# Restacked inputs in longer runs, input chunk 7 ahead of the taps, signed weights on GpSimd, small loads on SyncE, and identity matmuls in two waits

## The chip, the cores and the metric

The kernel runs on one NeuronCore of one Trainium2 chip. The metric is the device time of one execution in microseconds. Engines are named as in the profile: PE is TensorE, PEld its weight loads, DVE is VectorE, ACT is ScalarE, POOL is GpSimd, SP is SyncE, which here only issues DMAs.

## The reference, cut to what matters

A two-layer trunk over 256 tokens of width 1024, all in float32. Each layer is `x += mixer(rms_norm(x))`, then `x += moe(rms_norm(x))`; a final RMS norm follows.

- Layer 0's mixer is a diagonal complex state-space layer: `u = h @ w_in`; 64 groups of 16 channels with 64 complex states each; `y = real(C x) + d * u`; GELU; `g @ w_glu`, split into value and gate, `val * sigmoid(gate)`.
- Layer 1's mixer is differential attention with rotary positions: `q, k, v = h @ w_qkv`; two softmaxes per head, `attn = p0 - lam * p1`, where `lam` is a scalar, `exp(sum(lq1*lk1)) - exp(sum(lq2*lk2)) + lambda_init`, from four vectors of 64; the output of a head is RMS-normed with the gain `attn_subln_g`; then `@ w_o`.
- The MoE picks one of 4 groups and 2 of its 8 experts per token, 32 experts of width 256; gate, up and down weights of all 32 experts are read in each layer, 100 MB a layer.

## The kernel before, in words

Each engine has its own program, written out by hand in order; they meet in semaphores. An engine that waits holds up all that is behind it in its own order. SyncE issues nearly all DMAs, in one long order: inputs, state-space weights, the restacking, GLU and router weights, the expert stream of layer 0 (`whole`, L436 and L438), the eight 512-column pieces of the attention weights (`columns`, L414), the final gain (L532), then the expert stream of layer 1. Each expert unit has a slot; SyncE waits in `freed` until TensorE is done with the unit that was there. The stream of layer 0 begins when all four outputs of the state-space layer are written (`y_done` 4).

**The state-space layer.** TensorE computes u transposed in eight chunks of 128 channels (`inputs`, L1729); two chunks fill a PSUM bank. ScalarE copies a bank into SBUF in another order (`keep_u`, L685); SyncE writes it to DRAM (L449), waits, and reads it back as four loads of 64 KB into U4, each in runs of 64 elements (`restack`, L454). `drive(o)` (L1774) multiplies the transposed weights with U4, 32 recorded matmuls for each of four octets; ScalarE copies the result (`keep_x`, L398 and L399). VectorE scans: `local_states`, `carries` (both with `advance`, L1240 to L1243) and `carried` (L1284 to L1296), each for two halves; `skips` (L1249) adds the skip term to the taps' result in PSUM. `taps(o)` (L1792) multiplies the block weights with the output weights, of which `signed_c` (ScalarE, L693) makes the signed part Cb and `blocks_b` (L704) the blocks; `own` (L769) copies the taps' result into Fw. GpSimd computes eight dense weight pieces (L574 to L576), which ScalarE spreads (`spread_w2`, L780), and clears buffers (L556). The output is `y_taps` (L1834, U4 with Fw, opens the PSUM group) and `y_states` (L1841, the states with W2, closes it); then GELU (L825), a turn (L1849), a copy (L832) and the gated product `glu` (L1862).

**The attention's head.** When the last scatter of layer 0 is in PSUM, ScalarE and VectorE copy the halves of x (L624, L1511); ScalarE's `norm_raw` then makes the table of the square root resident (L625) and copies the turned x (`keep_tile`, L652). Ahead of `norm_raw` ScalarE issues five small loads: the four lambda vectors and the sub-norm gain, each to all 128 partitions (L586). TensorE runs `turn_tile` (L1681), `project(0, 0)`, `turn_tile`, `project(0, 1)`, then `turn_qk(0, 0)` (L2055), which needs VectorE's rotation (L1546 to L1550), and only then the other projections (L2045). VectorE waits for all five small loads (`s_att` 80) at L1526, ahead of its lambda arithmetic (L1528 to L1533) and the first rotation.

**The last scatter.** In layer 1 the down product of a pass (L2009, banks 6 and 7) is scattered one pass later in three bfloat16 parts (`scatter_parts`, L1974). For the last pass nothing stands between: VectorE and ScalarE split the rows (L1493 to L1502, L927 to L935), then come the scatter, the square sums (L599) and the final norm (L1069).

## Time and profile before

| | |
|---|---|
| runs | 792.18 us median of 3 (790.82 to 796.93) |
| profiled execution | 790.53 us, its span 788.7 us |
| busy, share of the span | PE 87%, PEld 51%, ACT 32%, DVE 37%, POOL 4% |
| mean granted TensorE clock | 0.95 of full |
| DMA | 238.43 MB, mean 302 GB/s |
| chain that ended last | PE 55%, SP's issues 17%, DMA 11%, DVE 9%, ACT 5% |

The profile's digits in 40 slices show where each resource works (a digit is the busy share of a slice of 19.7 us in tenths):

```profile
PE   4899999989976685686899999898989999994995
DMA  8544809979999999999990565048999932999981
```

A busy PE is not PE at its peak; its clock is either 1.2 GHz (0.50 of full) or 2.4 GHz (1.00), and a stretch with a value between has both. Idle time of an engine costs nothing unless the chain runs through it.

### The profile page before, as it was taken

Reading aid. Unit: us, or ns where it says so; the run is one execution under the profiler, and the core shown is the slowest. Engines: PE = TensorE matmul, PEld = TensorE weight load, DVE = VectorE, ACT = ScalarE, POOL = GpSimd, SP = SyncE. Lnnn points to the kernel's source line nnn. Section 1 sums busy time; section 2 is a strip of 40 time slices with the busy share of each in tenths; the row PEclk is TensorE's granted clock in tenths of the full one; section 3 lists DMA queues with packets and bytes.
Section 4 is the critical chain, followed back from the end, with each engine's and each line's share of the span. In section 5 each row is a group of like instructions: output and inputs, shape, how many; then the busy total and the mean of one; then the engine's idle time right before and its main releaser. Section 6 shows DMA issues by size and latency. Waiting matters only on the chain.

```text
span 788.7 us, 16095 instructions
## 1 busy us (share of the span) xinstructions
PE 684.7 (87%) x6372; PEld 405.5 (51%) x6372; DVE 291.6 (37%) x767; ACT 248.7 (32%) x582; POOL 35.1 (4%) x36
## 2 busy tenths in 40 slices
PE   4899999989976685686899999898989999994995
PEld 4888654555533343344444444555655655652562
DVE  6897751171111010010241535735334433331334
ACT  6686533261111011011311324533233322321224
POOL 1580000000000000000000000000000000000000
PEclk9996999999998798898999999999999999997998
DMA  8544809979999999999990565048999932999981
GB/s 225 165 134 149 230 2 396 361 308 374 418 422 420 422 419 420 421 420 411 381 385 32 214 227 199 2 179 327 421 419 422 419 162 112 423 421 420 421 338 53
DMA packets 66238, 238.43 MB, mean 302 GB/s; under 512 B 25840, under 2 KB 25984, under 8 KB 41600
## 3 DMA queue, kind: packets, MB, share of 16 engines
q1 hardware_dynamic: 65136, 237.34, 76.4%
q8 instruction: 42, 0.69, 0.3%
q10 hardware_dynamic: 1040, 0.24, 0.1%
q14 instruction: 20, 0.16, 0.1%
HBM read 235.47 MB, written 2.10 MB: 301 GB/s over the span
## 4 chain that ended last, share of the span: by engine, by line
PE 55%; SPq 17%; DMA 11%; DVE 9%; ACT 5%; issue 2%; ACTq 1%; DVEq 0%
SPq L438 14%; PE ps L1954 12%; PE ps L2045 10%; PE ps L1862 6%; PE ps L2009 6%; PE ps L1934 5%; DMA ring<-in_moe_w_up 4%; PE ps L1974 4%; DMA hT<-in_moe_w_up 4%; DMA ring<-in_moe_w_down 3%; SPq L436 3%; PE ps L2108 2%; PE ps L2119 2%; PE ps L1774 2%; PE ps L1841 1%
## 5 line engine op out<-in xcount | busy, mean ns | idle before, releaser
L1954 PE MATMUL ps<-ring,work 128*32 128x256 f32 x1504 | 126.5, 414 | 31.2 <-DMA ring<-in_moe_w_gate 11.5
L1954 PE MATMUL ps<-work 128*32 128x256 f32 x864 | 91.7, 410 | 25.1 <-DMA ring<-in_moe_w_up 7.7
L1954 PEld LDWEIGHTS ps<-ring,work 128*32 128x32 f32 x1504 | 71.2, 119 | 71.5 <-issue 50.4
L1474 DVE TENSOR_TENSOR work<-ps,work 128x256 f32<-128x256 f32 x21 | 12.9, 612 | 191.2 <-PE ps L1954 191.2
L1954 PEld LDWEIGHTS ps<-work 128*32 128x32 f32 x864 | 50.2, 118 | 56.4 <-issue 40.2
L2009 PE MATMUL ps<-ring,work 128*32 128x512 f32 x464 | 70.6, 610 | 4.7 <-issue 3.9
L1934 PE MATMUL ps<-work,xr 128*128 128x128 bf16 x736 | 66.5, 219 | 0.7 <-DVE work L1383 0.6
L1934 PE MATMUL ps<-work 128*128 128x128 bf16 x368 | 63.9, 219 | 0.0
L1934 PEld LDWEIGHTS ps<-work,xr 128*128 128x128 bf16 x736 | 57.6, 98 | 8.9 <-issue 3.3
L1862 PE MATMUL ps<-ring,work 128*128 128x512 f32 x128 | 57.1, 598 | 2.7 <-ACT work L832 2.3
L2045 PE MATMUL ps<-ring,hT 128*128 128x512 f32 x128 | 56.7, 596 | 1.8 <-ACT hT L652 1.8
L1974 PE MATMUL ps<-work 128*128 128x512 bf16 x168 | 40.4, 392 | 3.6 <-DVE work L1502 3.6
L911 ACT ACTIVATE work<-ps 128x256 f32<-128x256 f32 x21 | 13.3, 631 | 86.5 <-PE ps L1954 86.5
L1954 PE MATMUL ps<-hT,work 128*32 128x256 f32 x160 | 40.4, 410 | 0.0
L1862 PEld LDWEIGHTS ps<-ring,work 128*128 128x128 f32 x128 | 23.6, 190 | 31.0 <-issue 26.8
L2009 PE MATMUL ps<-work 128*32 128x512 f32 x176 | 36.3, 595 | 3.4 <-issue 2.5
L2045 PEld LDWEIGHTS ps<-ring,hT 128*128 128x128 f32 x128 | 23.7, 190 | 29.4 <-issue 27.1
L918 ACT COPY work<-ps 128x256 f32<-128x256 f32 x13 | 4.8, 372 | 100.2 <-PE ps L1965 100.2
L1934 PEld LDWEIGHTS ps<-work 128*128 128x128 bf16 x368 | 36.0, 98 | 0.0
L2009 PEld LDWEIGHTS ps<-ring,work 128*32 128x32 f32 x464 | 17.9, 112 | 34.2 <-issue 33.1
L896 ACT ACTIVATE work<-ps,work 128x128 f32<-128x128 f32 x92 | 26.2, 368 | 25.5 <-PE ps L1934 25.5
L1974 PEld LDWEIGHTS ps<-work 128*128 128x128 bf16 x168 | 15.7, 100 | 27.6 <-issue 7.5
(339 smaller groups left out, 1067.0 us busy)
## 6 DMA issues: line engine op xcount, KB each, us to landing
ring<-in_moe_w_down SPq DMA_DIRECT2D x22, 2048.0 KB, 24.4
ring<-in_moe_w_gate SPq DMA_DIRECT2D x21, 2048.0 KB, 19.8
ring<-in_moe_w_up SPq DMA_DIRECT2D x16, 2048.0 KB, 29.5
work<-in_moe_w_up SPq DMA_DIRECT2D x12, 2048.0 KB, 19.7
work<-in_moe_w_gate SPq DMA_DIRECT2D x9, 2048.0 KB, 29.0
work<-in_moe_w_down SPq DMA_DIRECT2D x8, 2048.0 KB, 23.0
ring<-in_ssm_w_glu SPq DMA_DIRECT2D x4, 2048.0 KB, 9.1
ring<-in_attn_w_qkv SPq DMA_DIRECT2D x4, 2048.0 KB, 27.2
```

Source lines behind the costliest of these rows:

```text
L436: sp.dma_start(halves[slot_of(i)][e], src[:, e, :]).then_inc(here, 16)
L438: sp.dma_start(places[slot_of(i)].rearrange("p (e n) -> p e n", e=2), src).then_inc(here, 16)
L896: ins = act.activation(xg[:, k, :], ps[:, 5, P * (k - 4):P * (k - 4) + P], ACT.Copy, scale=gq[:, 2 * l + 1, k:k + 1])
L1774: ins = mm(ps[:, V_AT[o] + r // 4, P * (r % 4) + 64 * i:P * (r % 4) + 64 * i + 64], W1T[o % 2][:, i, r, :], U4[:, OCT * o + r, :], start=T ...
L1862: ins = mm(ps[:, GLU_OUT[n] + half, :], gT[:, k, tt * P:(tt + 1) * P], win[u][:, k, :], start=(k == 0), stop=(k == KD - 1))
L1934: ins = mm(ps[:, 4 + k // 4, P * (k % 4):P * (k % 4) + P], parts[i][:, tt, k, :], sel[:, tt, :], start=(tt == 0 and i == 0), stop=(tt == T ...
L1954: ins = mm(ps[s, 6 + j // 2, 0:256], xg[:, k, s], pairs[slots[e // 2]][e % 2][:, k, :], start=(k == 0), stop=(k == KD - 1))
L1974: ins = mm(ps[:, 2 * tt + half, :], selT[:, P * tt:P * tt + P], low_half(half) if i == 2 else v[:, 512 * half:512 * half + 512], start=Fal ...
L2009: ins = mm(ps[s, 6 + half, :], hidT[:, P * k + 32 * e:P * k + 32 * e + 32], downs[slots[e // 2]][e % 2][:, k, 512 * half:512 * half + 512] ...
L2045: ins = mm(ps[:, qkv_bank(tt, c), :], hT[:, k, tt * P:(tt + 1) * P], win[slot][:, k, :], start=(k == 0), stop=(k == KD - 1))
L2108: ins = mm(ps[:, bank, :], oT[:, k, 0:P], win[slot][:, k, :], start=(k == 0), stop=(k == KD - 1))
L2119: ins = mm(ps[:, 2 + c, :], oT[:, k, P:2 * P], win[slot_of(unit(0, NQ, 6 + c))][:, k, :], start=(k == 0), stop=(k == KD - 1))
```

## The change

- Restacking: the staged copy is laid out so that the 128 elements of two chunks lie together, and each of the four loads reads runs of 128 elements; U4 then holds the pairs in another order, which `inputs_of` undoes.
- TensorE: `inputs(7)` and `turn_w1(3)` stand ahead of `taps(0)` and `taps(1)`; `y_states(0)` opens its group and `y_taps(0)` closes it.
- ScalarE: the signed weights are gone from it; `spread_w2(3)` and `keep_u(2)` stand ahead of `blocks_b`, and `own(0)` behind the weight copies. GpSimd makes the signed weights at the head of its dense chain.
- VectorE: `skips(0)` stands inside the carries of the first half.
- The five small loads of the attention go from ScalarE's queue to SyncE's, behind the attention weights; the square root's table is made resident ahead of the wait for the last scatter.
- `keep_clock(bank, n)` multiplies the identity with 512 columns of constants, n times, and nobody reads the result: three times behind `turn_tile(2, 0)`, seven times ahead of the last scatter.

```diff
@@ restack (SyncE)
-                rows = passing[b].rearrange("(q c) (k s m) -> c k q s m", q=4, k=2, s=SB)
+                rows = passing[b].rearrange("(q c) (s n) -> c q s n", q=4, s=SB)
                 for j in range(SB):
-                    dst = U4[32 * j:32 * j + 32, OCT * b:OCT * b + OCT, :].rearrange("c (k q) m -> c k q m", k=2)
-                    sp.dma_start(dst, rows[:, :, :, SB - 1 - j, :]).then_inc(u_in[b], 16)
+                    dst = U4[32 * j:32 * j + 32, OCT * b:OCT * b + OCT, :].rearrange("c (q k) m -> c q (k m)", k=2)
+                    sp.dma_start(dst, rows[:, :, SB - 1 - j, :]).then_inc(u_in[b], 16)
@@ SyncE, behind the attention weights
             sp.wait_ge(x_new, 2)
             sp.wait_ge(x_late, 2)
+            for n, name in enumerate(("q1", "k1", "q2", "k2")):
+                sp.dma_start(lam4[:, n, :], a["attn_lambda_" + name][0].partition_broadcast(P)).then_inc(s_att, 16)
+            sp.dma_start(subg, a["attn_subln_g"][0].partition_broadcast(P)).then_inc(s_att, 16)
             sp.dma_start(gains[:, 1, :], a["final_norm_g"].partition_broadcast(P)).then_inc(s_gain, 16)
@@ GpSimd
             pool.wait_ge(rest_clear, 1)
+            pool.wait_ge(c_ready, 2)
+            pool.wait_ge(cleared, 3)
+            for i in range(2):
+                for g in range(2):
+                    h = slice(64 * g, 64 * g + 64)
+                    pool.tensor_scalar(Cb[h, i, :, 16 * g:16 * g + 16], Cc[h, i, :, :], -1.0 if i else 1.0, None,
+                                       ALU.mult).then_inc(signed_ready, 1)
+                    pool.wait_ge(signed_ready, 2 * i + g + 1)
             pool.wait_ge(swapped_ready, 5)
-            pool.wait_ge(c_ready, 2)
@@ ScalarE
             def norm_raw(first):
+                act.activation(small[:, 40:41], con[:, C_TURN:C_TURN + 1], ACT.Sqrt)
                 act.wait_ge(scat1, first)
                 for tt in range(TT):
                     act.copy(x[:, tt, 512:1024], ps[:, 2 * tt + 1, :]).then_inc(x_late, 1)
-                act.activation(small[:, 40:41], con[:, C_TURN:C_TURN + 1], ACT.Sqrt)
...
-                    act.copy(staged[b][:, 256 * c:256 * c + 256].rearrange("p (s l h) -> p s l h", s=SB, l=SEG), src).then_inc(u_staged, 1)
+                    dst = staged[b].rearrange("p (s k l h) -> p k s l h", s=SB, k=2, l=SEG)[:, c]
+                    act.copy(dst, src).then_inc(u_staged, 1)
...
             spread_w2(2)
-            signed_c()
-            blocks_b()
             spread_w2(3)
             keep_u(2)
+            blocks_b()
             keep_w1T(2, 0)
             keep_w1T(2, 1)
-            own(0, (0, 1))
             keep_u(3)
             keep_w1T(3, 0)
             keep_w1T(3, 1)
-            own(0, (2,))
+            own(0, (0, 1))
             keep_x(2, (0, 1))
-            own(0, (3,))
+            own(0, (2, 3))
             keep_x(3, (0, 1))
...
             total = moe(0)
-            for n, name in enumerate(("q1", "k1", "q2", "k2")):
-                dma(lam4[:, n, :], a["attn_lambda_" + name][0].partition_broadcast(P), s_att)
-            dma(subg, a["attn_subln_g"][0].partition_broadcast(P), s_att)
             norm_raw(total + 1)
@@ VectorE, carries
-                    if half and h == 4:
-                        skips(1)
+                    if h == 4:
+                        skips(half)
@@ TensorE
+            def keep_clock(bank, n):
+                for _ in range(n):
+                    mm(ps[:, bank, :], ident, con[:, 0:512], start=True, stop=True)
...
+            def inputs_of(o, r):
+                return U4[:, OCT * o + 2 * (r % 4) + r // 4, :]
...
             inputs(6)
-            taps(0)
-            taps(1)
             inputs(7)
             turn_w1(3, 0)
             turn_w1(3, 1)
+            taps(0)
+            taps(1)
             drive(2)
             drive(3)
...
-            y_taps(0)
-            y_states(0)
+            y_states(0, True)
+            y_taps(0, False)
             y_taps(1)
...
                 if l == 1:
+                    pe.wait_ge(y0_ready, passes_through(pe, l))
+                    keep_clock(6, 7)
                     scatter_parts(passes_since(pe, NQ))
...
             turn_tile(2, 0)
+            keep_clock(0, 3)
             pe.wait_ge(hT_ready, 5)
             pe.wait_ge(hT_late, 5)
             project(0, 0)
```

## Rows read from the trace of the kernel before

**Rows 1.** Timeline of SP's issues at 118 us: start, length, line, what.

```profile
117.78 0.89 SPq L438 DMA_DIRECT2D ring<-in_moe_w_gate  x2
```

**Rows 2.** Busy by stretch: us, PE, PEld, DVE, ACT, POOL busy, PE clock, DMA share, GB/s.

```profile
65.00:82.00 17.00, 17.00 (x102) 16.88 (x103) 12.15 (x25) 11.16 (x30) 0.00 (x0) 0.50 0.58 193
178.00:363.00 185.00, 137.73 (x1544) 75.73 (x1536) 20.74 (x51) 21.04 (x50) 0.00 (x0) 0.90 1.01 416
362.80:368.60 5.80, 5.76 (x56) 3.14 (x60) 0.00 (x0) 0.00 (x0) 0.00 (x0) 0.50 1.01 420
...
727.10:730.60 3.50, 3.46 (x36) 1.92 (x40) 0.00 (x0) 0.00 (x0) 0.00 (x0) 0.51 1.03 428
```

**Rows 3.** Timeline of PE, 34 to 100 us; in brackets the idle time before.

```profile
42.88 3.76 PE L1774 MATMUL ps<-gains,ring 128*128 128x64 f32 x32 [0.90 <-issue]
46.48 5.40 PE L1729 MATMUL ps<-hT,ring 128*128 128x256 f32 x24
...
58.10 3.72 PE L1729 MATMUL ps<-hT,ring 128*128 128x256 f32 x16
...
64.36 13.36 PE L1774 MATMUL ps<-gains,ring 128*128 128x64 f32 x64 [1.67 <-ACT ring L752]
...
85.89 3.70 PE L1862 MATMUL ps<-ring,work 128*128 128x512 f32 x8
```

**Rows 4.** Timeline of SP's issues, 391 to 446 us.

```profile
391.40 10.55 SPq L414 DMA_DIRECT2D ring<-in_attn_w_o  x2
402.05 3.69 SPq L532 DMA_DIRECT2D gains<-in_final_norm_g  x1
437.17 8.52 SPq L438 DMA_DIRECT2D ring<-in_moe_w_gate  x2
```

**Rows 5.** DMA issues: count, KB each, median us from issue to landing.

```profile
gains<-passing SPq DMA_DIRECT2D x16, 64.0 KB, 2.5
...
gains<-in_final_norm_g SPq DMA_DIRECT2D x1, 512.0 KB, 15.7
...
work<-in_attn_lambda_k ACTq DMA_DIRECT2D x2, 32.0 KB, 6.9
work<-in_attn_subln_g ACTq DMA_DIRECT2D x1, 64.0 KB, 7.9
```

**Rows 6.** Timeline of ACT, 12 to 100 us.

```profile
24.47 1.07 ACT L732 COPY ring<-ps 128x512 f32<-128x512 f32 x2 [3.79 <-PE ps L1746]
...
49.36 2.59 ACT L693 ACTIVATE ring<-ring 64x512 f32<-64x512 f32 x4
...
56.67 0.65 ACT L685 COPY ring<-ps 128x256 f32<-128x256 f32 x2
...
78.38 2.51 ACT L780 COPY work<-work 64x512 f32<-64x512 f32 x4
80.91 1.28 ACT L825 ACT_TABLE_LOAD   x1
```

**Rows 7.** Timeline of DVE at the second skip term.

```profile
96.97 0.30 DVE L1249 TENSOR_TENSOR ps<-ps,work 128x128 f32<-128x128 f32 x1 [4.58 <-PE ps L1792]
```

**Rows 8.** Timeline of POOL, 0 to 30 us.

```profile
12.86 0.95 POOL L556 MEMSET xr<- 128x1024 f32 x1 [9.40 <-PE ps L1671]
27.24 1.10 POOL L574 TENSOR_TENSOR xr<-ring 128x512 f32<-128x512 f32 x1 [13.43 <-ACT ring L715]
```

**Rows 9.** Timeline of DVE and PE at the attention's head.

```profile
383.73 7.13 PE L2045 MATMUL ps<-ring,hT 128*128 128x512 f32 x16 [1.83 <-ACT hT L652]
...
395.03 0.29 DVE L1528 TENSOR_TENSOR work<-work 128x128 f32<-128x128 f32 x1
...
397.95 0.69 DVE L1550 TENSOR_TENSOR work<-work 128x512 f32<-128x512 f32 x1
...
398.70 0.66 PE L2055 MATMUL ps<-con,work 128*128 128x128 f32 x4
```

**Rows 10.** Timeline of PE, two scatters of layer 1, the second the last.

```profile
765.03 2.76 PE L1974 MATMUL ps<-work 128*128 128x512 bf16 x12
...
778.05 4.45 PE L1974 MATMUL ps<-work 128*128 128x512 bf16 x12 [3.56 <-DVE work L1502]
```

More of the change, by code:

```diff
@@ L308, in build @@
         bbar_ready, block_b, pow_ready = sem("bbar_ready"), sem("block_b"), sem("pow_ready")
-        swapped_ready, mu_first, mu_ready, mu4_ready, local_done = (
-            sem(n) for n in ("swapped_ready", "mu_first", "mu_ready", "mu4_ready", "local_done"))
+        swapped_ready, mu_first, mu_ready, mu4_ready, local_done, signed_ready = (
+            sem(n) for n in ("swapped_ready", "mu_first", "mu_ready", "mu4_ready", "local_done", "signed_ready"))
         d_ready, u_staged = sem("d_ready"), sem("u_staged")
@@ L684, in keep_u @@
                     src = ps[:, b, 256 * c:256 * c + 256].rearrange("p (h l s) -> p s l h", l=SEG, s=SB)
-                    act.copy(staged[b][:, 256 * c:256 * c + 256].rearrange("p (s l h) -> p s l h", s=SB, l=SEG), src).then_inc(u_staged, 1)
-            def signed_c():
-                act.wait_ge(cleared, 1)
-                for i in range(2):
-                    for g in range(2):
-                        h = slice(64 * g, 64 * g + 64)
-                        act.activation(Cb[h, i, :, 16 * g:16 * g + 16], Cc[h, i, :, :],
-                                       ACT.Copy, scale=(-1.0 if i else 1.0)).then_inc(c_ready, 1)
+                    dst = staged[b].rearrange("p (s k l h) -> p k s l h", s=SB, k=2, l=SEG)[:, c]
+                    act.copy(dst, src).then_inc(u_staged, 1)
             def blocks_b():
@@ L1303, in _ @@
                     link(TTo(skip, spread(con[:, C_SKIP:C_SKIP + PC], 1, KD), spread(dcol, 2, PC), ALU.mult))
-                    skips(0)
                     dve.wait_ge(mu4_ready, 3)
@@ L1774, in drive @@
                         ins = mm(ps[:, V_AT[o] + r // 4, P * (r % 4) + 64 * i:P * (r % 4) + 64 * i + 64], W1T[o % 2][:, i, r, :],
-                                 U4[:, OCT * o + r, :], start=True, stop=True)
+                                 inputs_of(o, r), start=True, stop=True)
                     if r % 4 == 3:
@@ L1783, in taps @@
                     pe.wait_ge(block_b, 8)
-                    pe.wait_ge(c_ready, 6)
+                    pe.wait_ge(signed_ready, 4)
                     pe.wait_ge(w1_ready, 8)
@@ L1827, in rows, with y_taps @@
                 return ps[64 * h:64 * h + 64, o, P * (r % 4):P * (r % 4) + P]
-            def y_taps(o):
+            def y_taps(o, begin=True):
                 pe.wait_ge(f_ready, 16 if o < 2 else 32)
@@ L1833, in y_taps, with y_states @@
                 for r in across:
-                    mm(rows(o, r), U4[:, OCT * o + r, :], Fw[:, OCT * o + r, :], start=(r % 4 == 0), stop=False, skip_group_check=True)
-            def y_states(o):
+                    ins = mm(rows(o, r), inputs_of(o, r), Fw[:, OCT * o + r, :], start=(begin and r % 4 == 0), stop=not begin, skip_group_check=True)
+                if not begin:
+                    ins.then_inc(y_done, 1)
+            def y_states(o, begin=False):
+                pe.wait_ge(v_in, 6 if o < 2 else 8)
                 pe.wait_ge(state, o + 1)
@@ L1840, in y_states @@
                     for r in across:
-                        ins = mm(rows(o, r), Xs[o][:, i, r, :], W2[:, i, OCT * o + r, :], start=False, stop=(i == 1),
-                                 skip_group_check=True)
-                ins.then_inc(y_done, 1)
+                        ins = mm(rows(o, r), Xs[o][:, i, r, :], W2[:, i, OCT * o + r, :], start=(begin and i == 0 and r % 4 == 0),
+                                 stop=(i == 1 and not begin), skip_group_check=True)
+                if not begin:
+                    ins.then_inc(y_done, 1)
             def turn_g(o):
```

## The prediction

> **What bounds the kernel now.** I read the busy table by stage first, then the chain of waits, then the order on each engine around the edited places. The span has four kinds of stretch. Up to 178 us the TensorE program sets the pace: DMA is idle for long parts of it, and the expert stream begins only at 117.8 us, when all of the state-space output is done [rows 1]. From 178 to 363 us DMA is the bound, at 1.01 busy and 416 GB/s [rows 2]; what restarts it is a buffer that TensorE frees, so every microsecond that TensorE is earlier at 178 us is handed on to 363 us. The attention (383 to 540 us) is TensorE again, and the second expert layer alternates between the two. A wait anywhere in the attention head or in front of 178 us therefore reaches the end one to one.
>
> Two places inside this matter. The last two drives (L1774 from 64.36 us) take 13.36 us for 64 recorded matmuls, where one drive of 32 took 3.76 us at 42.88 us [rows 3]: from 65 to 82 us the granted clock is 0.50, that is 1.2 GHz, after TensorE had stood still for 1.67 us between the last transposes of the weights and the third drive [rows 2, 3]. And at the attention head SyncE is far behind: its two loads of the output weights are issued from 391.40 to 402.05 us, each issue taking over 5 us because the queue ahead is full, and the final gain only at 402.05 us, landing 15.7 us later [rows 4, 5].
>
> **Part 1, the early order.** Before, chunk 7 (3.72 us) stood behind the taps, which had to wait for ScalarE's signed weights and block copies; the staging copy of chunks 4 and 5 was made at 56.67 us although the chunks were complete at 51.9 us (46.48 plus 5.40), since 2.59 us of signed weights and the blocks stood ahead of it [rows 3, 6]. Now the signed weights are on GpSimd and the staging copy stands ahead of the blocks: it runs at about 52, so the third restack starts some 4.7 us earlier than the end of the old copy (57.3) and lands by about 60. TensorE then does chunk 6 (to 56.2), chunk 7 (to 59.9), the transposes (1.0) and both taps (2.0) and is at the third drive at 62.9, not 64.36, with no idle ahead of it. The fourth drive needs the fourth restack: staging ends at 60.6 (chunk 7 at 59.9 plus 0.65), write and wait 2.0, four issues 2.6, landing 2.5 [rows 5], so 67 to 67.5; the third drive ends at 66.6. If the clock stays at full rate both are over at 70.9 instead of 77.7.
>
> What is late next: ScalarE. It has the remaining own-weight copies, the last input copies, then 2.51 us of L780 and a 1.28 us table load ahead of the first GELU [rows 6]. By its durations it is ready at 77.0; with turn and states behind it the first gated product starts at 80.2 instead of 85.89, 5.7 us earlier. If the clock falls in the fourth drive anyway, this is 82.0 (3.9 earlier), and if it falls as before, at 65, about 82.8 (3.1 earlier). The drives ran from 65 to 77.7 without bringing the clock back [rows 2], so a fall is as likely as not; I take 4.0. Putting the states ahead of the own-weight term hides that term's wait; putting the skip term of the first half into its carries makes VectorE wait about 1.1 us for the taps, but VectorE later stands 4.58 us waiting for TensorE [rows 7], which covers it. Nothing behind this place binds otherwise: the same chain of GELU, taps 2 and 3 and own weights follows TensorE.
>
> The 512-byte runs halve the pieces of the 16 restack loads, whose landing is 2.5 us [rows 5]; no row has such a load with longer runs. Between nothing and the 0.90 us that TensorE idled ahead of the second drive [rows 3], I take 0.4, a gain. The Trainium skill (DMA: Bandwidth & Descriptors, Specifications) says that transfers below 512 B are not moved at line rate; by it the gain would be nearer the 0.9, and the sum 0.5 lower. The trace shows only the short runs.
>
> GpSimd gets four one-input products of 512 elements per partition, from 25.54 us [rows 6]. A two-input product of 512 takes 1.10, a memset of 1024 takes 0.95 [rows 8]: 0.5 to 1.1 each, 2 to 4.4 in all, where its chain started at 27.24. It starts 0.3 to 2.7 us late. Its first piece (three operations, about 3.5 us behind the start) is then there by 33.5 instead of 30.8. What covers that is ScalarE's own order, in which two weight copies and other work stand ahead of each spreading. Nothing charged; if that cover is thin, up to 1 us, which is in the low end of the early gain. Early total: 4.4 us gained, from 2.5 to 7.
>
> **Part 2, the attention head.** The table load goes ahead of the wait: 1.28 us of it left the path, of which 0.9 counts (the transposes end only then). Three identity products come in. A float32 product of 512 columns is recorded as two matmuls, and 16 of them took 7.13 us [rows 9], so one costs 0.88 and three 2.6; TensorE is free at 381.9 (383.73 less its 1.83 of waiting), so projection 0 starts at 384.5 instead of 383.73, a loss of 0.8. But what follows makes both irrelevant.
>
> The four lambda vectors and the sub-norm gain were issued by ScalarE and landed 6.9 to 7.9 us later [rows 5]. Now SyncE issues them, in program order behind the eight attention weight loads and behind the wait for the new x. That wait is long over; the weight issues are not: the place where SyncE arrives is 402.05 us [rows 4]. VectorE waits for all five at 395.03, ahead of the first rotation; the rotation ends at 398.64 and TensorE's first q turn follows at 398.70, ahead of projections 2 to 5 in its order [rows 9]. In the place of these loads stood the final gain, which landed at 402.05 + 15.7 = 417.8, because what is queued ahead of it on the same queue has to drain first. I take 417.8 for the last of the five. VectorE is then 22.8 us late, TensorE has no other work in its order after projection 1, and the first turn comes at 421.5: **22.8 us lost**. Low end: every issue 0.45 and a landing of 7.9 as on ScalarE's queue [rows 5], 411.8, a loss of 16.7. High end: each issue as long as the 3.69 of the final gain, the last one from 416.8, landing in the 2.5 to 3 us of a short load on an empty queue: 420.2, a loss of 25.2. Behind SyncE's five issues stand the final gain (needed at the end only) and the second layer's stream, whose next issue waited until 437.17 anyway [rows 4].
>
> The standstill also lowers the clock. After the waits for weights TensorE worked 5.8 us and 3.5 us at 0.50 before it was full again [rows 2], half of it lost: 1.7 to 2.9, and 3.4 with a little more allowed at the top; I take 2.3. The attention's other waits are on TensorE itself, and the second layer's weight waits start from buffers that TensorE frees, so nothing of this is won back.
>
> **Part 3, the last scatter.** TensorE stood 3.56 us ahead of it, and its 12 bfloat16 matmuls then took 4.45 us, against 2.76 at full clock [rows 10]. Seven identity products at 0.86 to 0.88 take 6.0 us from 774.5, so to 780.6; the scatter starts 2.5 us later than 778.05 and is 1.7 faster. The first half is complete 1.3 later, the second about 0.8: **1.0 us lost**. Nothing at best, 6 more if the identities themselves ran at half clock.
>
> **Sum.** 790.5 - 4.4 + 22.8 + 2.3 + 1.0 = 812.2 us against the profiled execution (790.53, span 788.7). The median of the runs is 792.18, 1.65 above it: 813.8, so I say 813.
>
> **Rivals.** (a) *Queue order does not matter*: the five land 8 us after their issue, at about 411.8. For it: they are tiny, and that is what ScalarE's did [rows 5], while DMA was just as full. Against: the final gain on SyncE's own queue took twice that. 790.5 - 4.4 + 16.7 + 2.3 + 1.0 = 806.1, 808 by the median. The Trainium skill (DMA: Bandwidth & Descriptors, Issuing engines are not separate DMA queues) says that the issuing engine only saves the sequencer's time and that all run on the same 16 engines. Taken literally it speaks for this rival; the rows of the final gain and of ScalarE's loads disagree with it, 15.7 against 6.9 to 7.9 us.
> (b) *No stall*: not slower. Place: VectorE's wait at 395.03. It decides if SyncE reaches the loads by about 387, so that a landing of 8 us is in time; then only the small terms count: 790.5 - 4.4 + 0.7 + 1.0 = 787.8, 789.5 by the median. Against it is SyncE at 402.05; for it only that the early gain could loosen the queue, but the queue is full because DMA is the bound, and it shifts with it.
> (c) *The issues themselves block*: 3.69 each, the high end: 790.5 - 4.4 + 25.2 + 3.4 + 1.0 = 815.7, 817.4.
> (d) *The early gain is not there*, the clock falling as before and GpSimd late: 1 us instead of 4.4, 817.
>
> **Chances.** Forecast 0.55, (a) 0.18, (c) 0.10, (d) 0.10, (b) 0.07. Low end of the range: (a) with the full early gain of 7 and 1.7 for the clock, 803. High end: (c) with the early gain at 2.5 and 1.5 for the tail, 820. All but (b) are slower by far more than 1% (about what a measurement of this kernel can tell from no change); (b) lies within 1%, and would be faster by over 1% only with the whole 7 us: 0.02.
>
> **What would show it.** Late: a wait of VectorE's L1528 product of over 15 us for DMA of the lambda loads, these issued by SyncE right behind the output weights; a TensorE hole of over 20 us ahead of the first q turn, then half clock for some microseconds; DMA busy in the first half of that hole and empty behind it. Early: third drive near 63 us, first gated product 3 to 6 us earlier, the first expert load near 113 us. End: seven identities ending near the split's end plus 2.5 us, the scatter in 2.8 us. The forecast is wrong if the five loads overtake the weights, or if SyncE reaches them before VectorE does.

## The result, and the profile after

The changed kernel takes 813.55 us (median of 4 runs, 812.11 to 814.86); the kernel before took 791.5 us in the runs beside it. The ratio is 1.0231, with a 95% interval of 1.0198 to 1.0264: slower, by about 2%, and within a microsecond of the forecast of 813. The profiled execution took 812.98 us, its span is 810.4 us, 21.7 more than before. The 40 slices and the chain of waits of the changed kernel:

```profile
PE   4899999999867747768549998998999999984996
DMA  8546529969999999999930266118999952999971
...
PE 55%; SPq 21%; DMA 13%; DVE 4%; ACT 4%; issue 2%; POOL 1%; ACTq 1%; DVEq 0%; POOLq 0%
```

SyncE's issues are 21% of the chain where they were 17%, and slice 21 (405 to 425 us) has 0.4 for TensorE and 0.3 for DMA: both stand still for most of it.

**The attention's head.** SyncE's order, and then VectorE and TensorE at the place where the five small loads are needed (start, length, line, in brackets the idle time before it and what ended it):

```profile
397.94 3.70 SPq L533 DMA_DIRECT2D work<-in_attn_lambda_q  x1
401.68 2.75 SPq L533 DMA_DIRECT2D work<-in_attn_lambda_k  x1
404.48 0.64 SPq L533 DMA_DIRECT2D work<-in_attn_lambda_q  x1
405.15 0.64 SPq L533 DMA_DIRECT2D work<-in_attn_lambda_k  x1
405.83 0.64 SPq L534 DMA_DIRECT2D work<-in_attn_subln_g  x1
```

```profile
413.64 0.29 DVE L1524 TENSOR_TENSOR work<-work 128x128 f32<-128x128 f32 x1 [21.62 <-DMA work<-in_attn_subln_g]
```

```profile
417.31 1.12 PE L2066 MATMUL ps<-con,work 128*128 128x128 f32 x4 [21.57 <-DVE work L1546]
418.21 8.31 PE L2056 MATMUL ps<-ring,hT 128*128 128x512 f32 x16
426.37 0.60 PE L2066 MATMUL ps<-con,work 128*128 128x128 f32 x4
```

The 21.6 us split into three: VectorE is ready at 392.03 and SyncE comes to the loads 5.9 us later, at 397.94; the five issues take until 405.83 for the last to begin, 7.9 us, of which 6.45 are the first two; and that last one lands 7.8 us after its issue. The landings by the view of the DMAs (size, median from the start of the issue):

```profile
ring<-in_attn_w_o SPq DMA_DIRECT2D x2, 2048.0 KB, 19.9
...
gains<-in_final_norm_g SPq DMA_DIRECT2D x1, 512.0 KB, 8.0
...
work<-in_attn_subln_g SPq DMA_DIRECT2D x1, 64.0 KB, 7.8
```

The final gain, which took 15.7 us in the place of these loads [rows 5], now takes 8.0: the small loads stand in its place. From SyncE's arrival to the landing of the last of the five it is again 15.7 us (397.94 to 413.6). One by one, counted from the start of its issue, the five land after 12.0, 9.4, 7.8, 7.8 and 7.8 us, so from 409.9 to 413.6; the second load of the output weights, queued just ahead of them, is issued at 392.6 and lands 20.0 us later, at 412.6. The table of stretches (length; busy time and count of PE, PEld, DVE, ACT, POOL; granted clock, DMA share, GB/s) shows the hole and what follows it:

```profile
395.60:417.30 21.70, 0.14 (x1) 0.00 (x0) 3.17 (x9) 0.20 (x1) 0.00 (x0) 0.61 0.81 294
417.30:426.40 9.10, 9.09 (x21) 4.39 (x22) 2.05 (x4) 0.59 (x1) 0.00 (x0) 0.81 0.01 2
```

The turn and the projection behind the hole take 9.06 us (417.31 to 426.37), before 7.36: 1.7 us for the clock.

**The early stage.** TensorE, and GpSimd's new products:

```profile
35.76 0.60 PE L1761 MATMUL ps<-con,ring 128*128 128x128 f32 x4
38.02 3.79 PE L1779 MATMUL ps<-gains,ring 128*128 128x64 f32 x32 [1.65 <-ACT ring L754]
...
53.56 7.07 PE L1730 MATMUL ps<-hT,ring 128*128 128x256 f32 x32
...
63.40 3.79 PE L1779 MATMUL ps<-gains,ring 128*128 128x64 f32 x32
68.20 6.14 PE L1779 MATMUL ps<-gains,ring 128*128 128x64 f32 x32 [1.02 <-DMA gains<-passing]
...
82.91 3.27 PE L1871 MATMUL ps<-ring,work 128*128 128x512 f32 x7
```

```profile
25.55 6.20 POOL L573 TENSOR_SCALAR ring<-ring 64x512 f32<-64x512 f32 x4 [11.28 <-ACT ring L734]
```

Chunks 6 and 7 run together, the third drive is 1.0 us earlier than before and at full clock; the fourth falls to half clock (0.55 on average from 68.2 to 79.0 us). The first gated product is 2.98 us earlier than before [rows 3], and so is the first expert load (114.83, before 117.78 [rows 1]). The four signed products take 6.20 us, so the dense chain starts 4.6 us later (31.83, before 27.24), and TensorE waits 1.65 us ahead of the first drive, which it did not before.

**The tail**, TensorE from the seven identities on (the second view gives durations min/median/max, then the first and the last start):

```profile
794.78 6.28 PE L1710 MATMUL ps<-con 128*128 128x512 f32 x14
```

```profile
L1983 PE MATMUL ps<-work x11: 379/379/379, 801.1 to 803.3; 128*128 128x512 bf16 x11
```

The scatter runs at full rate (379 ns each), but starts 9.90 us after the start of the last down product (791.21); before, 7.20 (770.85 to 778.05 [rows 10]). The whole is 1.34 us longer.

**The sum by the trace**: -2.95 to the first expert load, -0.39 more to the attention's head, +0.38 in the head up to the first q turn, +21.57 for the hole, +1.70 for the clock, +0.05 to the last down product, +1.34 in the tail: 21.70 us, the difference of the spans.

### The profile page after: what moved, and what is told of

Read it like the earlier page. It is cut to its first block, busy times and chain, and to the rows that moved or that the text cites. A ratio compares the mean times of both kernels' runs of the same rounds, so it can differ in the third digit from the quotient of the medians.

```text
span 810.4 us, 16129 instructions
## 1 busy us (share of the span) xinstructions
PE 686.6 (85%) x6378; PEld 406.2 (50%) x6392; DVE 292.3 (36%) x767; ACT 246.4 (30%) x578; POOL 41.1 (5%) x40
## 4 chain that ended last, share of the span: by engine, by line
PE 55%; SPq 21%; DMA 13%; DVE 4%; ACT 4%; issue 2%; POOL 1%; ACTq 1%; DVEq 0%; POOLq 0%
PE ps L1963 11%; SPq L438 10%; PE ps L2056 9%; DMA hT<-in_moe_w_up 8%; SPq L414 7%; PE ps L1871 6%; PE ps L2018 6%; PE ps L1943 5%; DMA ring<-in_moe_w_down 3%; PE ps L1983 3%; SPq L436 2%; PE ps L2119 2%; PE ps L2130 2%; PE ps L1730 2%; PE ps L1779 2%
## 5 line engine op out<-in xcount | busy, mean ns | idle before, releaser
L1963 PE MATMUL ps<-ring,work 128*32 128x256 f32 x1504 | 123.5, 409 | 34.9 <-DMA ring<-in_moe_w_up 12.5
L1983 PE MATMUL ps<-work 128*128 128x512 bf16 x154 | 35.5, 379 | 2.1 <-issue 2.1
L1943 PEld LDWEIGHTS ps<-work 128*128 128x128 bf16 x368 | 36.0, 98 | 0.0
L2026 PE MATMUL ps<-work 128*128 128x512 f32 x64 | 29.6, 605 | 0.0
```

What stands on the lines that cost most here:

```text
L1943: ins = mm(ps[:, 4 + k // 4, P * (k % 4):P * (k % 4) + P], parts[i][:, tt, k, :], sel[:, tt, :], start=(tt == 0 and i == 0), stop=(tt == T ...
L1963: ins = mm(ps[s, 6 + j // 2, 0:256], xg[:, k, s], pairs[slots[e // 2]][e % 2][:, k, :], start=(k == 0), stop=(k == KD - 1))
L1983: ins = mm(ps[:, 2 * tt + half, :], selT[:, P * tt:P * tt + P], low_half(half) if i == 2 else v[:, 512 * half:512 * half + 512], start=Fal ...
L2026: ins = mm(ps[:, 2 * tt + half, :], swT[:, P * tt:P * tt + P], yy[:, 512 * half:512 * half + 512], start=False, stop=True, skip_group_chec ...
```

## The experiments

The ratios are against runs of the kernel before made beside each experiment, whose medians were 794.5 to 795.9 us (single runs 787.8 to 800.5), not the 791.5 beside the changed kernel. So ratios of experiments compare better than their times do, and against 791.5 the gains of the fastest kernels below would be half as large. "Small loads" are the four lambda vectors and the sub-norm gain.

### 1. The small loads back on ScalarE, the rest as changed

```diff
-            for n, name in enumerate(("q1", "k1", "q2", "k2")):      (SyncE)
-                sp.dma_start(lam4[:, n, :], ...).then_inc(s_att, 16)
-            sp.dma_start(subg, ...).then_inc(s_att, 16)
+            for n, name in enumerate(("q1", "k1", "q2", "k2")):      (ScalarE, ahead of norm_raw)
+                dma(lam4[:, n, :], ..., s_att)
+            dma(subg, ..., s_att)
```

> The changed kernel, but ScalarE issues the four lambda vectors and the sub-norm gain again, ahead of its norm. Theory (SyncE's place behind the attention weights is the whole loss): VectorE's wait of 21.6 us goes, and with it 1.7 us of half clock on the projection behind it; 813.5 - 23.3 = 790.2 us, ratio to before about 0.998, first q turn near 396 us. Rival (part of the hole comes from the other edits at the head, the identities or the table load): a wait of several us stays ahead of the first q turn and the time is above 795.

Measured: 791.46 us, ratio 0.9967 (0.9936 to 0.9997), span 789.6. The hole is gone: the first q turn stands right behind the projection, with no idle time ahead of it:

```profile
398.73 0.66 PE L2066 MATMUL ps<-con,work 128*128 128x128 f32 x4
```

It comes at 398.73 and not near 396 because this execution is 2.6 us later in its early stage already (first gated product at 85.53). The loads hold all of the slowness; the rest of the change holds none of it.

### 2. The small loads on SyncE, alone, in the kernel before

The same edit the other way round, and nothing else of the change.

> The kernel before with one part of the change only: the five small loads issued by SyncE behind the attention weights. Theory: VectorE's wait appears in full, 21 to 22 us from 395.0, then 1.5 to 2.5 us of half clock: 791.5 + 23.3 = 814.8 us, ratio 1.029. Rival (the loss needs the other parts, for instance the earlier stream): well under 810.

Measured: 815.6 us, ratio 1.0241 (1.0174 to 1.0308). SyncE's issues and VectorE's wait in this kernel:

```profile
405.69 3.69 SPq L533 DMA_DIRECT2D work<-in_attn_lambda_q  x1
409.42 2.75 SPq L533 DMA_DIRECT2D work<-in_attn_lambda_k  x1
...
413.58 0.64 SPq L534 DMA_DIRECT2D work<-in_attn_subln_g  x1
```

```profile
421.38 0.29 DVE L1528 TENSOR_TENSOR work<-work 128x128 f32<-128x128 f32 x1 [22.17 <-DMA work<-in_attn_subln_g]
```

The same 7.9 us of issuing and the same landing of 7.8 us (413.58 to 421.38) as in the changed kernel. One part of the change alone gives its whole slowness.

### 3. The small loads on SyncE, two transfers earlier

```diff
             for c in range(8):
+                if c == 6:
+                    (the waits for x_new and x_late, and the five small loads)
                 freed(unit(0, NQ, c))
```

> The changed kernel, with SyncE's five small loads two places earlier, ahead of the two loads of the output weights (with the wait for the new x). Theory (the wait is the sum of SyncE's arrival, of blocked issues and of a landing of 7.8 us, and moves with the place): issues from 387.3 to 395.2, landing by 403, VectorE waits 11 us instead of 21.6, 813.5 - 10.7 = 802.8 us. Rival (a small load on this queue lands only when all 2 MB loads that SyncE has queued are through, whatever its place): no earlier than before, 813.

Measured: 807.38 us, ratio 1.0161 (1.0094 to 1.0228).

```profile
389.00 5.23 SPq L529 DMA_DIRECT2D work<-in_attn_lambda_q  x1
394.28 0.55 SPq L529 DMA_DIRECT2D work<-in_attn_lambda_k  x1
...
396.88 0.64 SPq L530 DMA_DIRECT2D work<-in_attn_subln_g  x1
```

```profile
406.37 0.29 DVE L1527 TENSOR_TENSOR work<-work 128x128 f32<-128x128 f32 x1 [12.65 <-DMA work<-in_attn_subln_g]
```

SyncE is at the loads 8.9 us earlier than in the changed kernel, and the wait is 9.0 us shorter. The issues again take 7.9 us in all (389.00 to 396.88), though this time the first holds 5.23 of it; the landing is 9.5 us. SyncE now comes 4.7 us ahead of VectorE (ready at 393.73), so that of the 7.9 us of issues only 3.2 are in the wait. The last of the five lands 2.9 us behind the 2 MB load ahead of them (403.5, by its 19.9 us from issue to landing), and 5.4 us ahead of the output weights, so the rival fails. Expected were 802.8. Missing from the sum are 1.7 us of landing, 1.8 of an early stage that is later in this profile, and 0.9 of clock (turn and projection took 9.99 us, 410.04 to 420.03, where the changed kernel took 9.06).

### 4. The small loads at the same moment, but issued by ScalarE

```diff
             norm_raw(total + 1)
+            act.wait_ge(qkv_done, 2)
+            (the five small loads, issued by ScalarE)
```

> The changed kernel (813.55 us), with the five small loads issued by ScalarE instead of SyncE, but only behind its wait for the second projection, at about 395.7 us, some 2 us ahead of the moment at which SyncE came to them. SyncE's two blocked issues (3.70 and 2.75 us) should not occur here: the five are issued by 398, land 7.8 us after their issue, at about 405.7, VectorE waits about 13.5 us instead of 21.6, and the time is 805.5. Rival 1: the time in which the issues were blocked was the loads' own wait for the transfers ahead, whichever engine issues them; then they land at about 413 as before, the wait is 21 us and the time 813. Rival 2: an issue on ScalarE's queue lands late because ScalarE, too, is blocked for 3 us or more for each; the wait is then 17 us or more.

Measured: 808.56 us, ratio 1.0151 (1.0117 to 1.0184). ScalarE's issues, then VectorE's wait, then the DMAs' landings:

```profile
400.38 0.37 ACTq L593 DMA_DIRECT2D work<-in_attn_lambda_q  x1
...
402.22 0.45 ACTq L593 DMA_DIRECT2D work<-in_attn_subln_g  x1
```

```profile
409.87 0.29 DVE L1525 TENSOR_TENSOR work<-work 128x128 f32<-128x128 f32 x1 [13.24 <-DMA work<-in_attn_subln_g]
```

```profile
ring<-in_attn_w_o SPq DMA_DIRECT2D x2, 2048.0 KB, 20.6
...
gains<-in_final_norm_g SPq DMA_DIRECT2D x1, 512.0 KB, 16.3
work<-in_attn_lambda_q ACTq DMA_DIRECT2D x2, 32.0 KB, 5.7
...
work<-in_attn_subln_g ACTq DMA_DIRECT2D x1, 64.0 KB, 7.6
```

This settles that the queue is the cause, and not the moment. The wait is 13.24 us, as expected (13.5), and both rivals fail: VectorE is ready at 396.62, ScalarE comes 3.8 us later, the last issue starts 1.8 us behind the first and lands 7.6 us later. In the changed kernel these three were 5.9, 7.9 and 7.8 us. The issues take 0.37 to 0.45 us each instead of 3.70 and 2.75, which is 6 us of the wait (7.9 less 1.8). The five land 5.2, 5.8, 6.2, 7.1 and 7.6 us after their issue, the last at 409.8, while the second load of the output weights, issued on SyncE's queue at 397.4, is still in transfer until 418.0. So from ScalarE's queue they pass the large loads by 8.2 us; on SyncE's queue the last of them landed 1.0 us behind. The final gain, on SyncE's queue again in its old place, takes 16.3 us. The time is 3 us above the 805.5 expected; the profiled span, 807.0, is only 3.4 us below the changed kernel's, where 8 were expected. The trace shows two reasons: before the hole, this execution is 4.6 us later (its first projection at 385.57, against 380.96), and the clock behind the hole cost 2.95 us instead of 1.70 (turn and projection from 413.52 to 423.83). Some 1 us came back later.

### 5. Identities in the hole

In the changed kernel, `keep_clock(6, 22)` ahead of `turn_qk(0, 0)`.

> The changed kernel (813.55 us), with 22 identity products (19.4 us) ahead of the first q turn, so that TensorE works through most of the 21.6 us of standing still. They end about 2 us before the small loads are there. If the clock lost by the standstill is what the turn and the following projection pay (1.12 and 8.31 us instead of 0.66 and 7.03), these two return to 0.66 and 7.03, and the time is 1.7 us less, 811.8. Rival: the stall's length alone sets the time and the later work would take up 1.7 us anyway; then it stays at 813.5.

Measured: 815.29 us, ratio 1.0257 (1.0197 to 1.0316). TensorE's first drive in the early stage, and then the hole:

```profile
37.80 6.42 PE L1779 MATMUL ps<-gains,ring 128*128 128x64 f32 x32 [1.65 <-ACT ring L754]
...
400.20 19.05 PE L1710 MATMUL ps<-con 128*128 128x512 f32 x44
421.90 0.66 PE L2066 MATMUL ps<-con,work 128*128 128x128 f32 x4 [2.65 <-DVE work L1546]
422.39 7.03 PE L2056 MATMUL ps<-ring,hT 128*128 128x512 f32 x16
```

At the hole it is as expected: the turn takes 0.66 again and the projection 7.03, so the 1.7 us belong to the standstill and can be removed there. That they reach the end is not shown. The total did not fall, since the early stage of this execution, whose instructions are those of the changed kernel, was slower: the first drive took 6.42 us here and 3.79 there behind the same wait of 1.65 us, and the first gated product came at 87.50 instead of 82.91 us. From the first projection to the end it is 428.6 us against 429.4, only 0.8 less: 0.9 us of the 1.7 is lost again behind the hole. That much says nothing for the rival either, since the stretch from the second q turn to the end takes 383.2 to 385.3 us in the kernels with seven identities in the tail. A term of 1.7 us cannot be read from the totals of this kernel.

### 6. GpSimd's signed products later

The kernel of experiment 1, with the four products moved behind the fourth dense piece (their loop stands inside `for o in range(PAIRS // OCT)`, at `o == 2`).

> As the run with the small loads back on ScalarE, and GpSimd's four signed-weight products moved from the head of its dense chain to behind its fourth dense piece. Theory (at the head they delay the first dense piece by 4.6 us, ScalarE's first spreading waits 2.1 us for it, and the first drive starts 1.9 us late, of which 1.0 us reaches the later stages): the first drive is back at 36.1 us, the first gated product 1.0 us earlier than 82.9, and the time 1 us below that run, 789.2. Rival (other things bind there, VectorE or the restack): the first drive is earlier but the first gated product is not, 790.2.

Measured: 790.95 us, ratio 0.9941 (0.9916 to 0.9965), span 788.6. GpSimd:

```profile
41.20 6.20 POOL L574 TENSOR_SCALAR ring<-ring 64x512 f32<-64x512 f32 x4
```

The products take 6.20 us here too, so 1.55 us each is what they cost. The wait ahead of the first drive is gone (it starts at 35.65 and takes 3.68, right behind the transposes at 35.22), and the first gated product comes at 81.08, 1.8 us earlier than in the changed kernel. The interval overlaps that of experiment 1; as a gain it is not shown by the times, and the table of the next experiment has what the rows show.

### 7. Chunk 7 behind the taps again; restacking in short runs again

Both start from the kernel of experiment 6. One undoes the order (`taps(0)`, `taps(1)` ahead of `inputs(7)`; `blocks_b()` ahead of `spread_w2(3)` and `keep_u(2)`; the new places of `own(0)` and of `y_states(0)` stay), the other the restacking's layout (runs of 64 elements).

> The kernel with the small loads back on ScalarE and the signed products behind the fourth dense piece (790.95 us; first gated product at 81.08 us), with the order of chunk 7 and of ScalarE undone: taps ahead of chunk 7, block copies ahead of the third weight spreading and staging copy. If the order is what gains early, the third drive goes from 62.1 back to 64 to 65 us, behind a hole of 1 to 2 us, both last drives run at half clock (13 us together instead of 10), and the first gated product is at 84 to 86 us; the time rises by 1 to 4 us, as much as the second expert layer hands on. Rival: the earlier start came from the longer runs and GpSimd's share alone; then the first gated product stays within 1 us of 81.1 and the time is the same.

> The kernel with the small loads back on ScalarE and the signed products behind the fourth dense piece (790.95 us, restack landing 1.9 us from issue), with the restacking in runs of 64 elements as before. If the run length is what shortened the restack, four issues take 2.55 us again instead of 1.74 and the landing is 2.5 us again: each of the waits ahead of the second and the fourth drive is 1 to 1.4 us longer, the first gated product is 0.5 to 1.5 us later than 81.1 us, and the time up to 1.5 us more. Rival: the length does nothing and issues and landings stay at 1.74 and 1.9 us; the same time.

Measured: 790.02 us, ratio 0.9936 (0.9906 to 0.9966), for the order; 793.02 us, ratio 0.9982 (0.9951 to 1.0012), for the short runs. Executions differ by some 2 us before the first drive, so the early stage is best measured from the last transposes ahead of it to the first gated product:

| kernel | transposes at | gated product at | between |
|---|---|---|---|
| before | 35.70 | 85.89 | 50.2 |
| 2, only the small loads moved | 36.03 | 89.12 | 53.1 |
| changed | 35.76 | 82.91 | 47.2 |
| 1, loads back | 37.66 | 85.53 | 47.9 |
| 3, two transfers earlier | 37.59 | 84.70 | 47.1 |
| 4, loads late on ScalarE | 37.98 | 83.94 | 46.0 |
| 5, identities in the hole | 35.55 | 87.50 | 52.0 |
| 6, signed products later | 35.22 | 81.08 | 45.9 |
| 8, no tail identities | 35.49 | 81.15 | 45.7 |
| 8, three tail identities | 37.52 | 82.81 | 45.3 |
| 9, none in the head | 37.51 | 82.92 | 45.4 |
| 7, order undone | 37.76 | 82.96 | 45.2 |
| 7, short runs | 35.71 | 84.76 | 49.1 |

Kernels with the same instructions up to there stand together, and they show how far one execution can be trusted: 50.2 and 53.1 us for the order before; 46.0 to 47.9, and once 52.0, for the changed order (changed, 1, 3, 4, 5); 45.3 to 45.9 with the signed products later (6, both of 8, 9). So the early stage did get shorter, but its 3.0 us are one draw; and moving the signed products is worth some 1 to 2 us at this place (1.0 was expected).

The order of chunk 7 gains nothing: undone, the stretch is no longer (45.2 against 45.3 to 45.9), and the rival of that expectation holds. TensorE's third drive then follows without the hole that it had before, at full clock:

```profile
63.65 3.68 PE L1780 MATMUL ps<-gains,ring 128*128 128x64 f32 x32
69.11 5.15 PE L1780 MATMUL ps<-gains,ring 128*128 128x64 f32 x32 [1.78 <-DMA gains<-passing]
```

The third staged copy is written at 55.85 us there, 18.1 us behind the transposes; before it was 21.6 us (57.34), and 15.9 to 17.0 in the kernels with the new order and the later signed products (6, 8, 9). So the order is 1.1 to 2.2 us of what brought the third restack forward. For the other 3.5 us the signed weights that ScalarE no longer has ahead of it (2.59 us [rows 6]) are the likely main part; no run takes them alone. In the kernel with short runs the four loads of a restack are issued in 2.54 us instead of 1.74, and TensorE waits 0.9 us more ahead of the fourth drive:

```profile
42.81 4.56 PE L1779 MATMUL ps<-gains,ring 128*128 128x64 f32 x32 [0.81 <-issue]
47.17 7.98 PE L1730 MATMUL ps<-hT,ring 128*128 128x256 f32 x24
...
71.41 5.74 PE L1779 MATMUL ps<-gains,ring 128*128 128x64 f32 x32 [1.92 <-DMA gains<-passing]
```

But 3.4 us of its 49.1 are a lost clock from 43 to 54 us (4.56 for 3.76, 7.98 for 5.40), behind a wait of 0.81 that in experiment 6 was 1.04 and cost nothing. What is left is 45.7, as with long runs. The longer runs save 0.8 us of issuing for a restack and 0.4 us of landing (a median of 2.0 instead of 2.4 us), and shorten a wait; a gain at the gated product is not shown.

### 8. The tail: no identities, three identities

The kernel of experiment 6 with `keep_clock(6, 7)` taken out, and with `keep_clock(6, 3)` in its place.

> The kernel with the small loads back on ScalarE and the signed products behind the fourth dense piece, now without the seven identity products ahead of the last scatter (with them 790.95 us). My reading: the identities cost more than the clock gives back, since in the changed kernel the last part of the path (last down product to the end) came out 1.3 us longer than before. So here the scatter waits 3.6 us, takes about 4.4 us instead of 2.8, and the time is 1.3 us less, 789.6. Rival: the identities pay; then the time is 792 or more.

> The same kernel with three identity products ahead of the last scatter instead of seven. Three take 2.6 us of a wait of 3.6, so the scatter should start on time. If what came directly ahead keeps the clock up, it takes 2.8 us: 1.7 us less than without identities, about 788.3, and 2.5 less than with seven. Rival: the remaining 0.9 us of standing still is enough to lose the clock; then the scatter takes 4.4 us and the time is that of the kernel without identities, 789.6.

Measured: 787.62 us, ratio 0.9896 (0.9864 to 0.9927) without; 788.14 us, ratio 0.9919 (0.9883 to 0.9954) with three. The scatter without identities, and then with three (11 of its 12 recorded in both):

```profile
L1984 PE MATMUL ps<-work x11: 379/634/634, 775.2 to 779.0; 128*128 128x512 bf16 x11
```

```profile
L1984 PE MATMUL ps<-work x11: 379/379/379, 776.8 to 778.9; 128*128 128x512 bf16 x11
...
  DVE work L1499: 1.0, 1
```

From the start of the last down product to the end of the span it is 17.8 us without (767.77 to 785.6), 16.7 with three (769.35 to 786.1), 19.2 with seven (769.42 to 788.6) and 17.8 in the kernel before. By these rows, of one execution each, seven lose 1.3 us and three gain 1.1: they end 1.0 us before the split, and that wait didn't cost the clock. The totals of none and three do not tell them apart. Without identities the time fell by 3.3 us (from 790.95), more than the 1.3 expected; the tail explains 1.3 of it, and 1.65 more were there when the last down product began.

### 9. An identity ahead of the fourth drive; none in the head

Both start from the kernel with three tail identities: `keep_clock(4, 1)` in `drive(3)`, ahead of its wait for the restack; and `keep_clock(0, 3)` taken out of the head.

> The kernel with three tail identities (788.14 us), and one identity product (0.88 us) in the wait ahead of the fourth drive, which stood 0.4 to 1.1 us there. In the changed kernel the fourth drive ran at 0.50 from about 69 us on; in three other kernels it stayed at full clock and the first gated product came no earlier, because ScalarE is the one waited for. So I expect the time unchanged, 788, and the first gated product within 1 us of that kernel's. Rival: the clock of the drives is on the path; then the first gated product comes 2 us earlier and the time is 786.

> The kernel with three tail identities (788.14 us), without the three identity products ahead of projection 0. There TensorE would wait for ScalarE's turned tile instead of working 2.7 us: in the kernel before, the wait was 1.83 us. With the table load ahead of the wait the turned tile should be there about 0.5 to 1.3 us before the identities end; projection 0 starts that much earlier, and if the clock holds, the time is 0.5 to 1 us less, 787.4. Rival: the standstill of about 1.5 us costs the clock for some microseconds, as a fall elsewhere did; then the first projection takes 8 us or more instead of 7.03 and the time is the same or up to 1 us more.

Measured: 787.95 us, ratio 0.9928 (0.9901 to 0.9954), for the one more; 788.97 us, ratio 0.9932 (0.9901 to 0.9962), without those in the head. The fourth drive held its clock (66.37 3.68 us), but it did so in five of the kernels without that identity as well (3.76 us, those of experiments 1, 4 and 8 and the one without head identities), and the stretch of the table above is 45.6 us, no shorter. Behind the drives TensorE waits 2.14 us for VectorE (L1296) and 1.64 us for ScalarE, so the drives are not on the path, as expected. In the head:

```profile
378.98 1.33 PE L1678 MATMUL ps<-con,x 128*128 128x128 f32 x8 [0.79 <-DVE x L1508]
381.54 8.62 PE L2057 MATMUL ps<-ring,hT 128*128 128x512 f32 x16 [1.23 <-ACT hT L660]
```

Without identities TensorE waits 1.23 us, the clock falls, and the projection takes 8.62 us: the rival of that expectation holds, and the time is no less. From one turn to the next it is 11.0 us (378.98 to 389.99), with the identities 10.4 in the changed kernel and 10.6 in the one of experiment 6, before 9.9, where a wait of 1.83 left the clock at 1.00. The identities win 0.4 to 0.6 us against a fall, and lose 0.5 to 0.7 where there is none.

## Why the prediction was right, point by point

- **Direction and size**: 813 against 813.55. The sum was -4.4 +22.8 +2.3 +1.0; the trace has -3.0 (-2.95, -0.39 and +0.38), +21.6, +1.7 and +1.3. The mechanism of each is there. That both sums come to 21.7 is luck: the measured terms differ from the forecast ones by +1.4, -1.2, -0.6 and +0.3. And the early stage alone varies by more than a microsecond between executions, so an agreement within one is luck too; what the prediction had right is that one stall of some 22 us decides.
- **The stall (22.8, measured 21.6)**. Place, waiting engines and what is queued behind came as predicted, and experiments 1 and 2 show that it is the whole slowness. The 15.7 us from SyncE's arrival to the landing, carried over from the final gain, came out exactly (in experiment 2 too). Of the 1.2 us of error 1.1 are where SyncE stands: 7.0 us behind VectorE in the kernel before (402.05 and 395.03), 5.9 in the changed one.
- **Why 15.7 again**. The prediction had it that what is queued ahead on the same queue must drain first. The landings bear that out for the last of the five: it landed 1.0 us behind the second load of the output weights (413.6 and 412.6), and 1.1 us in experiment 2; in the kernel before, the final gain landed 1.15 us behind it (417.75 and 416.6, from an issue at 396.7 and 19.9 us to landing). It is no strict order, for the first of the five landed 2.7 us ahead of that load. The other description, blocked issues (7.9 us) and then a landing of 7.8 us as on ScalarE's queue, gives the same sum, and no run tells the two apart. Experiment 4 shows that the queue matters: from the first issue to the last landing it is 9.4 us on ScalarE's queue instead of 15.7, beside the same large loads. Rival (a) had the landing right and the issues wrong (1.8 us instead of 7.9); rival (c) had the blocking right for two issues of five. The Trainium skill (DMA: Bandwidth & Descriptors, Issuing engines are not separate DMA queues) says that another issuing engine saves only the sequencer's time. Counted from its issue the last load's landing agrees, 7.6 us from ScalarE and 7.8 from SyncE. But the sequencer's time is just what was on the path here: 7.9 against 1.8 us from the first issue to the last.
- **Slips in the working**, none of which moves the forecast. The high end, 420.2, does not follow from its own terms (416.8 and 2.5 to 3 us are 419.3 to 419.8). The low end of the range, 803, lacks the 1.65 us between median and profiled execution that all other times have (804.5). Rival (b) charges 0.7 us for the head where the text has 0.8.
- **The clock behind it (2.3, measured 1.7)**: 2.6 and 2.95 in experiments 3 and 4, behind shorter holes. Experiment 5 shows at the hole that it is the standstill's.
- **Early (4.4, measured 3.0 with the head's 0.4 in it)**. The mis-sized term is GpSimd's: I bounded its one-input products by 0.5 to 1.1 us each; they took 1.55, outside the bounds, and "nothing charged" was a wait of 1.65 us ahead of the first drive. Third and fourth drive came 0.5 and 0.7 to 1.2 us later than worked out (63.40 and 68.20), and the clock fell in the fourth, as I had called as likely as not. The step on chunk 7 named the wrong part: by experiment 7 its place brings nothing; ScalarE's relief from the signed weights is left as the cause, which was argued, not tried alone. The 0.4 us for the longer runs is not shown at the gated product, and nor is the 0.9 that the prediction gave beside it.
- **Head (0.8 lost, measured 0.4)**, **tail (1.0 lost, measured 1.3)**: near enough, and neither decides the result. The tail's loss is confirmed by experiment 8; the head's depends on whether the clock falls without the identities (experiment 9).
- **Rival (b)**, no stall: its time of 789.5 is nearly that of experiment 1 (791.46), where the loads are in time.

What stays open: why the early gain shrinks on its way. In experiment 6 the first expert load is 4.8 us earlier than before, the second layer's stream 2.7 us, the last down product 1.4 us. Such losses of 1 to 2 us come and go between the profiles (from the first expert load to the first of the attention weights: 225.4 to 228.6 us), and no run isolates them.

## What to carry to other kernels

A small load that is needed soon belongs on a queue without large transfers ahead of it, or ahead of them in the order (here two transfers earlier won 9 of 21.6 us; further ahead was not tried): look where the issuing engine stands when the load would have to be issued, count its blocked issues, and add the landing. A landing counted from the start of an issue holds the blocked time; subtract the issue's own duration before carrying it to another queue. Work that only keeps the clock has to end before what it waits for: by the rows of the tail three identities gained 1.1 us where seven lost 1.3. The best version here leaves the small loads where they were and the tail without identities (0.9896) or with three (0.9919, not told apart); it also has the signed products later.

## What the runs showed of the hardware

- On SyncE's queue behind 2 MB loads, a load of 32 KB took 3.70, 2.75 or 5.23 us to issue; five took 7.9 us in four kernels. On ScalarE's queue at the same place they took 0.37 to 0.45 us each. The 512 KB load of the final gain on SyncE's queue took 3.69 us to issue directly behind the 2 MB loads and 0.64 behind the five small ones.
- The same instructions with the same idle time lose TensorE's clock in one execution and keep it in another: 1.65 us ahead of the first drive (6.42 against 3.79 us for it). Nor does the longer wait lose it more surely: 1.83 us ahead of the first projection kept it and 1.23 lost it; ahead of the second drive 0.90, 1.04 and 1.47 us kept it, 0.81 and 0.93 lost it. Longer holes did not cost more: 1.5 to 1.7 us behind 21.6 and 22.1 us, 2.6 and 2.95 us behind 12.6 and 13.2 us. The Trainium skill (TensorE: Matmul & The Clock Gate, What's actually happening) says that the number of slow matmuls at the start of a kernel varies from run to run, and advises against fitting a particular count. The falls here are in the middle of a kernel, and what they cost varies too, by 2.6 us on one drive.
- Four one-input float32 products on GpSimd of 64 partitions by 512 elements took 6.20 us, 1.55 us each, in both places; a two-input product of 128 by 512 took 1.1 us.
